# Two transformer blocks on one core: conditioning sums folded by 32x32 transposition and seven grouped matmuls, another order of the opening loads, and the first two columns behind two norms run as a pair

## The reference, cut to what matters

```
mod = silu(c) @ w_ada + b_ada                     # 2048 x 12288: six vectors of 2048
sh1, sc1, ga1, sh2, sc2, ga2 = split(mod, 6)
h = rms_norm(x, g1) * (1 + sc1) + sh1
mixed = [bidirectional mLSTM (4 heads) | neighbourhood attention (8 heads)](h @ w_in) @ w_out
x = x + ga1 * mixed
h = rms_norm(x, g2) * (1 + sc2) + sh2
x = x + ga2 * conv_glu(h)                         # w_up, w_down
x = rms_norm(x, g_final)
for i in 0, 1:                                    # second block
    shift, scale, gate = split(silu(c_2) @ ada_w_2[i] + ada_b_2[i], 3)
    h = rms_norm(x, pre_g[i]) * (1 + scale) + shift
    y = spatial-gating mixer(h) if i == 0 else latent attention mixer(h)
    x = x + gate * rms_norm(y, post_g[i])
```

## Time and profile before

| | |
|---|---|
| median of 3 runs | 2559.79 us (2558.49 to 2563.99) |
| the profiled execution, its own time | 2558.37 us |
| its span in the profile | 2556.6 us |
| TensorE matmul busy | 2389.7 us, 93% |
| VectorE busy | 1980.4 us, 77% |
| ScalarE busy | 1118.8 us, 44% |
| mean granted TensorE clock | 0.985 of full |

### The profile page before, as it was taken

One profiled execution on the slowest core, in us unless ns is written; L12 is line 12 of the kernel. 1 busy time (PEld: TensorE's weight loads), 2 busy tenths in 40 slices (PEclk: granted clock), 3 DMA queues, 4 the chain that ended last, 5 costly groups with the idle time before them and its releaser, 6 DMA issues.

```text
span 2556.6 us, 33044 instructions
## 1 busy us (share of the span) xinstructions
PE 2389.7 (93%) x13438; PEld 2077.7 (81%) x13438; DVE 1980.4 (77%) x2463; ACT 1118.8 (44%) x1376; POOL 11.3 (0%) x12
## 2 busy tenths in 40 slices
PE   1499999998999999999997999999999997999996
PEld 1488887886888888888886888888888885888985
DVE  7988898798888777777787878677777676675765
ACT  1143344544454433444444434544444333455542
POOL 0000000000000000000000000000000000000000
PEclk9999999999999999999998999999999998999998
DMA  8979766685777688666684888766777773664342
GB/s 333 360 272 339 250 226 229 211 299 204 262 260 258 227 284 283 231 239 241 230 267 159 308 310 298 258 225 225 259 254 262 263 273 107 240 214 148 131 166 99
DMA packets 118297, 620.13 MB, mean 243 GB/s; under 512 B 13313, under 2 KB 14465, under 8 KB 75393
## 3 DMA queue, kind: packets, MB, share of 16 engines
q1 hardware_dynamic: 69840, 446.19, 49.7%
q10 hardware_dynamic: 48304, 171.82, 18.6%
HBM read 615.86 MB, written 2.10 MB: 242 GB/s over the span
## 4 chain that ended last, share of the span: by engine, by line
PE 87%; DVE 9%; issue 2%; ACT 1%; DMA 1%; POOL 0%; POOLq 0%; SPq 0%; ACTq 0%; DVEq 0%
PE pm L511 30%; PE ps L511 15%; PE pm L512 15%; PE ps L512 8%; PE pm L552 2%; PE pm L554 2%; PE pm L553 2%; DVE acc_first L1346 2%; PE pv L488 1%; DVE w_lo L1290 1%; PE ps L552 1%; PE ps L554 1%; PE ps L553 1%; DVE nt L1375 1%; DVE h L1381 1%
## 5 line engine op out<-in xcount | busy, mean ns | idle before, releaser
L1290 DVE TENSOR_TENSOR w_lo<-raw,w_hi 128x2048 fp32r<-128x2048 f32 (+2 forms) x412 | 892.1, 2165 | 327.0 <-ACT w_hi L896 326.1
L511 PE MATMUL pm<-h,w_hi 128*128 128x512 f32 x2526 | 896.8, 399 | 22.1 <-DVE h L1381 18.3
L896 ACT ACTIVATE w_hi<-raw 128x2048 fp32r<-128x2048 f32 (+2 forms) x412 | 746.3, 1812 | 387.3 <-DMA raw<-in_w_down 136.7
L512 PE MATMUL pm<-h,w_lo 128*128 128x256 f32 x2526 | 706.0, 280 | 0.0
L511 PEld LDWEIGHTS pm<-h,w_hi 128*128 128x128 f32 x2526 | 476.6, 189 | 139.0 <-issue 19.6
L512 PEld LDWEIGHTS pm<-h,w_lo 128*128 128x128 f32 x2526 | 478.4, 189 | 0.2
L511 PE MATMUL ps<-h,w_hi 128*128 128x512 f32 x1314 | 464.3, 396 | 0.0
L1305 DVE SCALAR_TENSOR_TENSOR acc<-ada,csil,acc 128x512 f32<-128x512 f32 x600 | 449.7, 749 | 13.4
L512 PE MATMUL ps<-h,w_lo 128*128 128x256 f32 x1314 | 366.0, 279 | 0.0
L511 PEld LDWEIGHTS ps<-h,w_hi 128*128 128x128 f32 x1314 | 246.5, 188 | 59.7 <-issue 2.2
L512 PEld LDWEIGHTS ps<-h,w_lo 128*128 128x128 f32 x1314 | 247.3, 188 | 0.1
(11 more groups left out here) (365 smaller groups left out, 2901.1 us busy)
## 6 DMA issues: line engine op xcount, KB each, us to landing
ada<-in_ada ACTq DMA_DIRECT2D x320, 512.0 KB, 5.4
raw<-in_w_up SPq DMA_DIRECT2D x88, 1024.0 KB, 4.9
raw<-in_w_in SPq DMA_DIRECT2D x56, 1024.0 KB, 6.3
raw<-in_w_down SPq DMA_DIRECT2D x64, 704.0 KB, 5.5
raw<-in_sgu_v SPq DMA_DIRECT2D x32, 1024.0 KB, 5.1
raw<-in_sgu_u SPq DMA_DIRECT2D x32, 1024.0 KB, 5.1
raw<-in_sgu_z SPq DMA_DIRECT2D x32, 1024.0 KB, 4.9
raw<-in_sgu_out SPq DMA_DIRECT2D x32, 1024.0 KB, 4.9
```

The costliest lines, as they stand in the source:

```text
L511: pe.matmul(dst[:, :], wh[:, k, :], hl, start=(kc == 0), stop=False, skip_group_check=True)
L512: mm = pe.matmul(dst[:, 0:T], wl[:, k, :], hi, start=False, stop=last, skip_group_check=True)
L896: act.activation(w_hi[:, q % HSLOTS, 0:n], raw[:, q % SLOTS, 0:n], ACT.Copy).then_inc(hi_ready, 1)
L1290: tt_(w_lo[:, q % SLOTS, 0:n], raw[:, q % SLOTS, 0:n], whole(w_hi[:, q % HSLOTS, 0:n]), ALU.subtract).then_inc(lo_ready, 1)
```

## The change

1. **Sum of a unit.** `sums` and its table `SUM_AT` are gone, and so is `take` for the forty later units. Instead, behind the eighth block of a unit VectorE transposes `acc` in 32 x 32 blocks into the weight buffer just used, and reduces each run of 32 values: 128 x 512 becomes 128 x 16 in `fold`, in which the 128 partitions have become four partial sums a column. For whole vectors at once, TensorE then adds the four parts and puts them on the right partitions: `fold_group`, four matmuls with a 0/1 matrix `sel` as the weights, at seven places (`FOLDS`), and VectorE takes each group with one `take_group`.
2. **Opening.** SyncE loads `par` and then at once the weight blocks; `gw` comes behind the first unit, `x` and `ident` behind the second, `mask_a` and the new `sel` last. VectorE no longer waits for the mean squares of norm 1: TensorE sums them straight from eight squared pairs, after the third unit, and VectorE computes the root's input after the sixth.
3. **Norms.** The last of the eight pairs of squares is no longer added on VectorE; TensorE sums it in two matmuls of its own, and the earlier seven in two more that need not wait for it. The result lies in `px[0]` (`pn`) and not in `ps`. `modulation` of norm 2 stands ahead of the reciprocal.
4. **First columns.** For `w_up0` and `lat` the first two columns run as a pair (`column_pair`): at each chunk of `h` both take their step. In `sgu_v` the first block waits chunk by chunk, not for four.

The core of the diff:

```diff
-        if _p % APIECES == APIECES - 1:
-            SUM_AT.setdefault(_at + 2, []).append(_p // APIECES)
-            TAKE_AT.setdefault(_at + 3, []).append(_p // APIECES)
+FOLDS = [(GA1, 1), (SH2, 2), (GA2, 1), (S0, 2), (G0, 1), (S1, 2), (G1, 1)]
...
             sp.dma_start(par[:, :], a["par"]).then_inc(const_in, 16)
-            sp.dma_start(ident[:, :], a["ident"]).then_inc(const_in, 16)
-            sp.dma_start(flat(x[:, :, :]), a["x"]).then_inc(x_in, 16)
-            sp.dma_start(flat(gw[:, :, :]), a["gate_w"]).then_inc(mix_const_in, 16)
-            sp.dma_start(flat(mask_a[:, :, :]), a["mask_a"]).then_inc(mix_const_in, 16)
             for u in range(FIRST_UNITS):
+                if u == 1:
+                    sp.dma_start(flat(gw[:, :, :]), a["gate_w"]).then_inc(mix_const_in, 16)
+                if u == 2:
+                    sp.dma_start(flat(x[:, :, :]), a["x"]).then_inc(x_in, 16)
+                    sp.dma_start(ident[:, :], a["ident"]).then_inc(ident_in, 16)
...
-            def sums(q):
-                for u in SUM_AT.get(q, ()):
-                    pe.wait_ge(ada_used, u * APIECES + APIECES)
-                    pe.wait_ge(unit_taken, u)
-                    for c in range(UCOLS // P):
-                        mm = pe.matmul(pv[:, c:c + 1], acc[:, u % 2, c * P:(c + 1) * P], ones[:, 0:1], start=True, stop=True)
-                    mm.then_inc(unit_summed, 1)
+            def fold_group(n):
+                v, count = FOLDS[n]
+                if n == 0:
+                    pe.wait_ge(sel_in, 16)
+                    pe.wait_ge(unit_taken, FIRST_UNITS)
+                else:
+                    pe.wait_ge(fold_taken, n)
+                pe.wait_ge(ada_used, (v + count) * UNITS * APIECES)
+                s = v * UNITS % FOLD_UNITS
+                src = fold[:, s:s + count * UNITS, :].rearrange("p u (c j) -> p (u c) j", j=P // BLOCK)
+                for j in range(P // BLOCK):
+                    lo = P - BLOCK - BLOCK * j
+                    mm = pe.matmul(pv[:, 0:count * KC], sel[:, lo:lo + P], src[:, :, j], start=(j == 0), stop=(j == 3))
+                mm.then_inc(fold_summed, 1)
...
                 for j in range(2):
-                    mm = pe.matmul(ps[:, half * T:(half + 1) * T], ones[:, :], src[:, j, :], start=(j == 0), stop=(j == 1))
+                    pe.matmul(pn[:, half * T:(half + 1) * T], ones[:, :], total[:, j, :], start=(j == 0), stop=False)
+                if half:
+                    pe.wait_ge(sqg_ready, PAIRS)
+                else:
+                    pe.wait_ge(sq_ready, SQUARED[name])
+                for j in range(2):
+                    mm = pe.matmul(pn[:, half * T:(half + 1) * T], ones[:, :], last[:, j, :], start=False, stop=(j == 1))
                 mm.then_inc(ss_ready, 1)
...
             def stage_columns(stage, need=None):
-                for c in range(COLUMNS[stage][0]):
-                    columns(stage, c, both(h), need if c == 0 else None)
+                if need is not None:
+                    column_pair(stage, both(h), need)
+                for c in range(2 if need is not None else 0, COLUMNS[stage][0]):
+                    columns(stage, c, both(h))
...
+                if k == APIECES - 1:
+                    chain.link(ins)
+                    turned = ada[:, p % ASLOTS, 0:UCOLS]
+                    chain.link(dve.transpose(turned, acc[:, :]))
+                    ins = dve.tensor_reduce(fold[:, u % FOLD_UNITS, :], turned.rearrange("p (j b) -> p j b", b=BLOCK), AX.X, ALU.add)
```

More of the change, by code:

```diff
@@ L121 @@
 PAIRS = KC // 2
-NORMS = ["norm1", "norm2", "final", "post0", "post1"]
-ADDED = {n: PAIRS * (i + 1) for i, n in enumerate(NORMS)}
+NORMS = ["norm2", "final", "post0", "post1"]
+ADDED = {n: (PAIRS - 1) * (i + 1) for i, n in enumerate(NORMS)}
+SQUARED = {n: PAIRS * (i + 1) for i, n in enumerate(NORMS)}
 SUMS = {n: i + 1 for i, n in enumerate(["norm1", "norm2", "final", "finalg", "post0", "pre1", "kv", "q", "post1"])}
@@ L458, in _ @@
                     sp.dma_start(buf, a["ada"][u * APIECES + k]).then_inc(ada_full[k], 16)
+            sp.dma_start(flat(mask_a[:, :, :]), a["mask_a"]).then_inc(mask_in, 16)
+            sp.dma_start(sel[:, :], a["sel"]).then_inc(sel_in, 16)
             for q, (stage, j) in enumerate(STAGE_OF):
@@ L550, in tokens @@
                             kc = 4 * part + k
+                            if need is not None and tt == 0:
+                                need(kc)
                             h_hi, h_lo = h[:, kc, tt * P:(tt + 1) * P], h[:, kc, T + tt * P:T + (tt + 1) * P]
@@ L697, in w_in_after @@
                 if (part, j) in B_WAVES:
+                    if B_WAVES[part, j] == 0:
+                        fold_group(0)
                     b_wave(B_WAVES[part, j])
@@ L757, in _ @@
                     pe.wait_ge(pre_sq, c // 2 + 1)
-                mm = pe.matmul(ps[:, 0:T], ones[:, :], pre_bufs[c // 2 % 4][:, c % 2, :], start=(c == 0), stop=(c == KC - 1))
+                mm = pe.matmul(pn[:, 0:T], ones[:, :], pre_bufs[c // 2 % 4][:, c % 2, :], start=(c == 0), stop=(c == KC - 1))
                 if c % 2:
@@ L1324, in begin @@
                     urgent()
-                for u in TAKE_AT.get(q, ()):
-                    take(u)
                 for p in ADA_AT.get(q, ()):
@@ L1395, in _ @@
             dve.memset(gates[0:GROW, :, :], 0.0)
-            clear_squares()
-            for p in range(PAIRS):
-                add_squares("norm1", p)
-            dve.wait_ge(gw_hi_ready, 1)
-            tt_(gw_lo[:, :, :], gw[:, :, :], whole(gw_hi[:, :, :]), ALU.subtract).then_inc(gw_lo_ready, 1)
-            rsqrt_mean("norm1", D)
             dve.wait_ge(silu_c, 1)
@@ L1542, in _ @@
             clear_squares()
+            take_group(0)
             for c in range(KC):
@@ L1592, in _ @@
                         final_squares(j // 4 - 1)
+                    if half == 0 and j == 0:
+                        take_group(2)
                     if j % 2:
                         residual(down, j // 2, GA2)
-                if half == 1:
-                    final_squares(PAIRS - 1)
             k = H_NORMS.index("pre0")
+            take_group(3)
             modulation("pre0", "pre", 0, C0)
@@ L1822, in constants @@
         cst[m % ROPE, 1024 + m] = 1.0
-    return {"ident": np.eye(P, dtype=f), "mask_a": mask_a.reshape(P, -1), "wmask": np.concatenate([win, win]), "mla_cst": cst}
+    sel = np.zeros((P, 2 * P - BLOCK), f)
+    sel[np.arange(P), P - BLOCK + np.arange(P) % BLOCK] = 1.0
+    return {"ident": np.eye(P, dtype=f), "sel": sel, "mask_a": mask_a.reshape(P, -1), "wmask": np.concatenate([win, win]), "mla_cst": cst}
 def blocks(w, k=KC):
```

106 lines of the change are left out of this document (73 added, 33 removed).

## The result

The changed kernel takes 2519.43 us (median of four runs, 2519.24 to 2523.24), the kernel before 2559.14 in the same comparison. The ratio is 0.9844, with a 95% interval of 0.9827 to 0.9861: 1.6% faster, 39.7 us. I had said 2506, range 2494 to 2522. The sign is right and the range holds it, but a quarter of the forecast gain is missing. In the profiled executions the span goes from 2556.6 to 2521.4, 35.2 us, against a forecast of 53.8.

What follows compares the result with a forecast made beforehand. TensorE was taken as the bound outside the opening and norms, VectorE and DMA in the opening. Terms 33.3 + 1.5 + 10.5 + 7.2 + 1.0 + 3.8 - 3.5 = 53.8 us gave 2504.6, or 2506 as median; range 2494 to 2522.

Steps and rivals of the forecast that it cites:

- Part 1: Forty unit sums at 0.9 us leave TensorE; seven folding groups replace them, three in the stream: -33.3 us.
- whatever leaves its queue there leaves the time: Outside the opening and norms TensorE never waits, so work removed there shortens the kernel while VectorE keeps up.
- Part 2: Behind `w_down0`, TensorE's 2.12 us of nothing ahead of a sum mostly goes: -1.5 us.
- Part 3: In the opening, VectorE starts on weight blocks sooner and ends at 98.0 instead of 108.7: -10.5 us.
- Part 4: Column three of `w_up0` and `lat` starts once its weights are there, 3.6 us each: -7.2; `sgu_v` another -1.0.
- Part 5: Shorter chains in norm 2, `post0`, `post1` and the final norm: -3.8 us, of which the final norm -1.3.
- Part 6: VectorE's added work, +1.3 us a unit, mostly hidden; `w_out` loses 1.5 and the attention stages 2: +3.5 us.
- VectorE takes part of it back: A dear transposition (2 us) slows `w_out`, the `w_in` stages and norms: 15 us back, 2521; chance 0.2.

Runs made afterwards that it cites:

- e6: The changed kernel plus forty dead sums on TensorE (four one-column matmuls each, never read or waited for), at the old sums' places: 2541.68 us.
- e2: The changed kernel without the column pairs in `w_up0` and `lat`, and with `sgu_v`'s first block waiting for four chunks at a time: 2527.02 us.
- e5: The changed kernel without VectorE's transposition and reduction behind each unit, so forty units add nothing to the modulation: 2508.88 us.
- e10: The changed kernel with one, two or three dead float32r matmuls of 64 columns at 41 places from `w_up0` on: one profiled execution, 2520.97 us.
- e3: The changed kernel with another table of blocks, fewer in `qb` and `vb` and 14 spread over `oa`: 2518.23 us.

## Why the prediction was right in sign and too high in gain

- **Part 1, sums leave TensorE.** The rows' price was right (a sum 0.89; the folding group in the stream costs 0.89 too: `w_down0`'s first piece takes 4.77 us for 3.88). The step that failed is "whatever leaves its queue there leaves the time". It supposed that the matmuls that stay keep their pace of 0.35. Taking the sums away left the columns in the slow pattern: 14.9 us more for the same steps, shown by e6, where idle sums alone take 11.2 of excess away. Net a sum was worth 0.56 us.
- **Part 2.** The stall behind `w_down0` is gone, as predicted; the 1.5 us can't be told apart there from the pattern.
- **Part 3, the opening.** Right: last unit ended at 98.25, 10.4 us earlier.
- **Part 4, pairs.** Right in mechanism and nearly in size (6.8 by e2's stages for 8.2). What I missed is that the lead was of use: 1.3 us of waits for `w_lo` later in `w_up0`.
- **Part 5, norms.** `post0` and `post1` are 0.7 shorter each (0.75 predicted). In norm 2 the last square begins 0.8 us late, since a `split` runs on VectorE to 597.85 ahead of the residual; with the pair the gain to the third column is 3.7 where 3.6 + 0.95 was predicted. The final norm stayed at full clock (1.03 us for the last four rows of the trace, where before's took 2.08), and its gain is in the 3.8 us of `sgu_v`, where 1.3 + 1.0 was predicted.
- **Part 6, VectorE.** The unit's price was right (711 + 686 ns, less a `take`), its place half right: `w_out` lost 2.7 us (1.5 predicted), the attention stages 5.6 (2 predicted), and `w_up0`, for which nothing was put, 2.5, by e5. The mechanism in attention was named ("a late VectorE delays a head's next step at once"), but its 2 us came from no row. In `vb` TensorE waits 2.0 us for `vb`'s values already before, at a granted clock of 0.97 over the stage; after, it waits 3.9, and 1.1 for `w_lo`, at 0.95:

```profile
PE px L680 <- ACT vb L1024: 2.0, 1, 2.0
396.90:455.80 58.90, 56.85 (x254) 47.08 (x253) 51.49 (x64) 25.70 (x31) 0.00 (x0) 0.97 0.65 230
```

The Trainium skill (VectorE: DVE Perf Modes, Rules for kernel authors) says to consider restructuring a reduction on the hot path, since it is the slowest Vector operation. e5 agrees that work added where VectorE is nearly full costs time, in `vb` and `w_out`. That the reduction is the slowest isn't so here, and the earlier trace rows could have told me: 686 ns against 689 for an addition of two operands of that size; `scalar_tensor_tensor` takes 749 (L1353).

The sum: the profiled gain is 18.6 us short of the forecast. The pattern accounts for 14.9 and VectorE for 10.8 - 3.5 = 7.3, 22.2 together. Of the 3.6 over, `sgu_v` has 1.5, which it gained beyond the forecast; the rest isn't assigned. By the medians the gain is only 14.1 short, and how the pattern stood in the executions that weren't profiled isn't known.

That the range held has luck in it. The range reached up to 2522 for the rival "VectorE takes part of it back". That rival had nearly the right time (2521) for the wrong reason: its dear transposition is not there, and nothing in the range stood for the pattern.

## What to carry to other kernels

When you plan to remove small work from a stream that an engine works through without waiting, look at the differences of the starts of single instructions ahead of and behind it, not at a mean. The price of the removed work is what it takes less what it changes in the pace of the rest. When a region has one engine nearly full, count the sum of its work over the region; moving it within the region mostly moves the wait. A lead that seems idle (a low half ready 3.6 us early) is spent once; ask which later wait it was covering.

## What the hardware showed that I had not expected

The same two matmuls, with weights, at the same full clock, run at a mean of 0.3467, 0.350 or 0.3533 us, in repeating patterns (0.350 and 0.343; 0.351 and 0.349; 0.350, 0.361, 0.349) that last up to a whole stage of 44 columns (`w_up1` in after) and turn, both ways, at an interruption as short as one 64-column matmul (e10, at three places fast to slow, at five slow to fast). Over this kernel that is up to 15 us, 0.6%, with no wait in any view. What in TensorE keeps such a round going stays open: the trace shows starts, not the queue behind them. And a wait can cost twice. In `vb` TensorE does next to nothing from 412 to 415 us, and for the 7 us behind it the granted clock is 0.51, that is 1.2 GHz and 3.4 us lost, before it is 2.4 GHz again:

```profile
412.00:415.00 3.00, 0.03 (x1) 0.00 (x0) 2.45 (x4) 2.38 (x3) 0.00 (x0) 1.00 0.94 300
415.00:422.00 7.00, 6.12 (x15) 4.88 (x16) 6.86 (x10) 4.98 (x8) 0.00 (x0) 0.51 0.50 167
422.00:425.00 3.00, 3.00 (x15) 2.46 (x14) 2.93 (x6) 0.00 (x0) 0.00 (x0) 1.00 0.03 14
```

These are stretches of the changed kernel. With the blocks moved out of `vb` (e3) the wait there is 0.8 us and the clock stays at 1.00 of full.
